# A two-block transformer kernel: a closing joined to the stage before it, and closings that begin the next stage's first products by token halves

## The reference

```
# block 1
mix = (g_a * o_a + g_b * o_b) @ w_out            # gated sum, then a product
h = h + rms_norm(mix, norm_mix_post)             # residual
hn = rms_norm(h, norm_mlp_pre)                   # input of the MLP
ff = square(relu(hn @ w_ff1)) @ w_ff2
h = h + rms_norm(ff, norm_mlp_post)
# block 2
a = rms_norm_2(h, ln_mix_pre);  proj = a @ w_in
... mix = concat(y_a, y_b, y_c, y_d) @ w_out
h = h + rms_norm_2(mix, ln_mix_post)
a = rms_norm_2(h, ln_ffn_pre)
h = h + rms_norm_2((silu(a @ w_gate) * (a @ w_up)) @ w_down, ln_ffn_post)
```

## Time and profile before

| | us |
|---|---|
| median of 3 runs (1671.85 to 1675.81) | 1674.38 |
| the profiled execution, whole | 1672.46 |
| its span, first to last instruction | 1670.6 |
| TensorE busy in the span | 1526.5 |
| VectorE busy | 813.0 |
| ScalarE busy | 572.4 |
| GpSimd busy | 284.7 |

### The profile page before, as it was taken

How to read it: one execution, slowest core, us unless ns; L and a number is a source line. 1 busy time by engine, 2 the same in 40 slices (tenths; PEclk the granted TensorE clock), 3 DMA queues, 4 the chain that set the end, 5 groups by cost and what they waited for, 6 DMA issues and landing times. The chain is left out here.

```text
span 1670.6 us, 18447 instructions
## 1 busy us (share of the span) xinstructions
PE 1526.5 (91%) x7440; PEld 1231.4 (74%) x7440; DVE 813.0 (49%) x1178; ACT 572.4 (34%) x894; POOL 284.7 (17%) x293
## 2 busy tenths in 40 slices
PE   7989699776997899999999799988798999999997
PEld 5878588664676688888887566767576888888885
DVE  4232433437753554434335597477856334334425
ACT  4221334433652441413133522176434222212212
POOL 0000000000020599100001167614322000000000
PEclk9999899887998999999999899989889999999998
DMA  4322121220013122332222312102012222222222
GB/s 170 101 77 79 51 76 45 95 76 1 1 51 113 63 91 99 101 101 102 92 88 82 101 51 77 57 26 77 1 51 76 76 99 84 95 101 101 101 88 76
DMA packets 37033, 129.23 MB, mean 77 GB/s; under 512 B 4644, under 2 KB 20924, under 8 KB 25300
## 3 DMA queue, kind: packets, MB, share of 16 engines
q1 hardware_dynamic: 36660, 127.93, 22.5%
q10 hardware_dynamic: 288, 0.12, 0.0%
HBM read 124.82 MB, written 3.17 MB: 77 GB/s over the span
## 5 line engine op out<-in xcount | busy, mean ns | idle before, releaser
L223 DVE TENSOR_TENSOR ring_lo<-ring_raw,ring_hi 128x2048 fp32r<-128x2048 f32 (+3 forms) x115 | 267.6, 2330 | 212.3 <-ACT ring_hi L213 212.2
L242 PE MATMUL bank<-xT_hi,ring_hi 128*128 128x512 f32 (+2 forms) x880 | 348.9, 397 | 5.3 <-PEq L1483 3.6
L242 PE MATMUL bank<-xT_lo,ring_hi 128*128 128x512 f32 (+2 forms) x880 | 345.7, 393 | 0.0
L242 PE MATMUL bank<-xT_hi,ring_lo 128*128 128x512 f32 (+2 forms) x880 | 345.5, 393 | 0.0
L213 ACT CAST ring_hi<-ring_raw 128x2048 fp32r<-128x2048 f32 (+3 forms) x115 | 212.7, 1852 | 254.8 <-DMA ring_raw<-in_w_ff 130.7
L242 PEld LDWEIGHTS bank<-xT_hi,ring_hi 128*128 128x128 f32 (+2 forms) x880 | 166.3, 189 | 46.8 <-issue 11.6
L242 PEld LDWEIGHTS bank<-xT_hi,ring_lo 128*128 128x128 f32 (+2 forms) x880 | 166.2, 189 | 36.5
L242 PEld LDWEIGHTS bank<-xT_lo,ring_hi 128*128 128x128 f32 (+2 forms) x880 | 166.6, 189 | 35.3
L242 PE MATMUL bank<-ring_hi,hid_hi 128*128 128x512 f32 x432 | 169.5, 392 | 3.9 <-DVE ring_lo L223 3.9
L242 PE MATMUL bank<-ring_hi,hid_lo 128*128 128x512 f32 x432 | 169.0, 391 | 0.0
L242 PE MATMUL bank<-ring_lo,hid_hi 128*128 128x512 f32 x432 | 169.0, 391 | 0.0
(11 more groups left out here) (496 smaller groups left out, 2133.0 us busy)
## 6 DMA issues: line engine op xcount, KB each, us to landing
ring_raw<-in_w_ff SPq DMA_DIRECT2D x32, 1024.0 KB, 4.8
ring_raw<-in_w_up SPq DMA_DIRECT2D x22, 1024.0 KB, 4.8
ring_raw<-in_w_proj SPq DMA_DIRECT2D x8, 1024.0 KB, 5.0
ring_raw<-in_w_gates SPq DMA_DIRECT2D x8, 1024.0 KB, 4.9
ring_raw<-in_w_fm SPq DMA_DIRECT2D x12, 512.0 KB, 4.8
ring_raw<-in_w_dn_a SPq DMA_DIRECT2D x6, 1024.0 KB, 4.9
ring_raw<-in_w_proj SPq DMA_DIRECT2D x8, 512.0 KB, 4.6
ring_raw<-in_w_out SPq DMA_DIRECT2D x4, 1024.0 KB, 5.0
```

Of the source, the lines that this page charges most:

```text
L223: k.nc.vector.tensor_tensor(k.ring.lo[:, g % SLOTS, 0:n], k.raw[:, g % SLOTS, 0:n], plain(k.ring.hi[:, g % SLOTS, 0:n]), ALU.subtract).the ...
L242: mm = k.nc.tensor.matmul(out, x, y, start=first and n == 0, stop=last and n == 3 * len(pairs) - 1)
```

## The change

Four things are done.

1. **mix1 joins the stage of the gated sum** (`stage_gemm(..., closing=closing)`), as mlp1 and mlp2 already do. The barrier between goes; in its place stand waits for the freed banks (`held`), for the first 14 taken tiles before phase one and for the last low part (`gated_low`) before phase two. SyncE's queue waits for the last taken tile before it issues S5's constants and the two gain rows. The closing's scratch tiles move to other addresses.
2. **The banks are numbered differently**: `bank(t, c)` is `2 * t + c` instead of `4 * c + t`, so that banks 0 and 1 belong to group 0 and are free first.
3. **Closings begin the next products** (`ahead`): mix1 and mix2 begin two tiles, mlp1 one tile of 96 columns. The first half of the tokens (256 columns of `xT`) of the first tile is made before `turn(2)`, that of the second before `turn(3)`; the second halves come behind `turn(3)` (and behind S5's transposes), in the same order. The next stage leaves out its first one or two steps (`begun`, `if i < 1`). For this the first two chunks of `w_ff1` are cut by columns, 256 columns over all of the depth, by two DMAs of 512 KB each, instead of 512 columns over half of it.
4. **Closings split one chunk more** before they end: ScalarE and VectorE make the parts of the next stage's second chunk inside the closing.

```diff
     def bank(self, t, c):
-        return self.k.pb[4 * c + t]
+        return self.k.pb[2 * t + c]
@@ Closing.sync
+        if after is not None:
+            sp.wait_ge(*after)
         if self.aside is not None:
             self.aside.load(sp)
-        if after is not None:
-            sp.wait_ge(*after)
@@ Closing.pe
-                        pe.wait_ge(*held[4 * c + t])
+                        pe.wait_ge(*held[2 * t + c])
...
         if self.pre is not None:
-            turn(2)
+            half = S // 2
+            if self.ahead:
+                wait_chunk(k, pe, self.end)
+                pe.wait_ge(self.low.sem, self.low.base + 4)
+            for n in range(2):
+                if n < len(self.ahead):
+                    self.begin(n, 0, half)
+                turn(2 + n)
             if self.aside is not None:
-                pe.wait_ge(self.low.sem, self.low.base + 2)
-                self.aside.turn(pe, self.bank(0, 0))
-            turn(3)
+                pe.wait_ge(self.low.sem, self.low.base + 6)
+                self.aside.turn(pe, self.bank(2, 0))
+            if self.ahead:
+                pe.wait_ge(self.low.sem, self.low.base + 8)
+            for n in range(len(self.ahead)):
+                self.begin(n, half, S).then_inc(self.ahead_done.sem, 1)
+
+    def begin(self, n, a, b):
+        _, _, out, pairs, _, _ = self.ahead[n]
+        return products(self.k, out[:, a:b], [(x, y[:, a:b]) for x, y in pairs], True, True)
@@ Closing.act, Closing.dve (at their ends)
+            if self.ahead:
+                split_hi(k, act, self.end + 2)
+            if self.ahead:
+                split_lo(k, dve, self.end + 2)
@@ first_block, the gated sum
-    stage_gemm(k, steps, gated, lambda j: "dve", act_each=split_sum, dve_tail=last_low, pool=add)
+    k.s5_in = S5Inputs(k)
+    begun, _, _ = gemm(k, g + 4, KD, 8, feature_tiles(k.xT, (0, P), 2 * P), 0)
+    closing = Closing(k, "mix1", g, ..., (134, 138, 142, 146, 120), pre=0, aside=k.s5_in,
+                      ahead=(begun, k.sig("gemm_done")),
+                      needs={(0, 0): (free.sem, free.base + KD + 6), (1, 0): (ended.sem, ended.base + 1)})
+    stage_gemm(k, steps, gated, lambda j: "dve", act_each=split_sum, dve_tail=last_low, pool=add, closing=closing)
-    g = stage_closing(k, Closing(k, "mix1", g, ..., (104, 108, 112, 116, 120), pre=0, aside=k.s5_in))
@@ stage_gemm
+                if i < begun:
+                    continue
@@ order_weights
-        whole("w_ff1", range(4 * q, 4 * q + 4))
+        if q == 0:
+            for half in range(2):
+                add_weights(k, *columns_of(d, "w_ff1", (0, 1), 4, 512, 256 * half, 256 * half + 256))
+        whole("w_ff1", range(4 * q + (2 if q == 0 else 0), 4 * q + 4))
```

More of the change, by code:

```diff
@@ L511, in stage_gemm @@
 def stage_gemm(k, steps, evac, owner=None, act_each=None, dve_each=None, dve_tail=None, pool=None,
-               needs=(), closing=None, opening=None):
+               needs=(), closing=None, opening=None, begun=0):
     nc = k.nc
@@ L1150, in __init__ @@
     def __init__(self, k, tag, g, lhs, phases, gain_name, at, pre=None, part=None, needs=None, out=None, aside=None,
-                 lead=None):
+                 ahead=None, lead=None):
         self.k, self.first, self.lhs, self.phases, self.pre = k, g, lhs, phases, pre
@@ L1155, in __init__ @@
         self.part, self.needs, self.out, self.aside = part, needs or {}, out, aside
+        self.ahead, self.ahead_done = ahead or ((), None)
         self.gain_row = k.d[gain_name]
@@ L1344, in act @@
             if self.aside is not None:
-                self.aside.keep(act, self.bank(0, 0))
+                self.aside.keep(act, self.bank(2, 0))
+            if self.ahead:
+                split_hi(k, act, self.end + 2)
     def pool(self, pool):
@@ L1701, in first_block @@
     gate_made = k.sig("gate_made")
-    free, summed, high = k.sig("gemm_free_dve"), k.sig("gated_sum"), k.sig("gated_high")
+    free, summed, high, ended = k.sig("gemm_free_dve"), k.sig("gated_sum"), k.sig("gated_high"), k.sig("gated_low")
     def low(dve, f):
@@ L1735, in last_low @@
         low(dve, KD - 2)
-        low(dve, KD - 1)
-    stage_gemm(k, steps, gated, lambda j: "dve", act_each=split_sum, dve_tail=last_low, pool=add)
+        low(dve, KD - 1).then_inc(ended.sem, 1)
+    k.s5_in = S5Inputs(k)
+    begun, _, _ = gemm(k, g + 4, KD, 8, feature_tiles(k.xT, (0, P), 2 * P), 0)
+    closing = Closing(k, "mix1", g, lambda f, t: mixT[:, f, t * P:(t + 1) * P], FULL_DEPTH, "norm_mix_post",
+                      (134, 138, 142, 146, 120), pre=0, aside=k.s5_in, ahead=(begun, k.sig("gemm_done")),
+                      needs={(0, 0): (free.sem, free.base + KD + 6), (1, 0): (ended.sem, ended.base + 1)})
+    stage_gemm(k, steps, gated, lambda j: "dve", act_each=split_sum, dve_tail=last_low, pool=add, closing=closing)
+    g = closing.end
     gate_made.base += 2 * KD
@@ L1741, in first_block @@
     high.base += KD
-    k.s5_in = S5Inputs(k)
-    g = stage_closing(k, Closing(k, "mix1", g, lambda f, t: mixT[:, f, t * P:(t + 1) * P], FULL_DEPTH, "norm_mix_post",
-                                 (104, 108, 112, 116, 120), pre=0, aside=k.s5_in))
+    ended.base += 1
     H = FF1 // P // MLP1_PARTS
@@ L1754, in first_block @@
         f0 = j
-        for _ in range(H // 4):
+        for n in range(H // 4):
+            if part == 0 and n == 0:
+                for _ in range(2):
+                    s, j, g = gemm(k, g, KD, 8, feature_tiles(k.xT, (0, P), 2 * P), j)
+                    steps += s
+                continue
             s, j, g = gemm(k, g, KD, 4, feature_tiles(k.xT, range(0, 512, P), 512), j)
@@ L1769, in first_block @@
     taken = k.sig("gemm_free_dve").base
+    begun2, _, _ = gemm(k, g + 4, KD, 8, feature_tiles(k.xT, (0,), 96, m=96), 0, range(4))
     closing = Closing(k, "mlp1", g, lambda f, t: hid[:, f, t * P:(t + 1) * P], FULL_DEPTH, "norm_mlp_post",
-                      (152, 120, 124, 156, 104), pre=1, part=y,
+                      (152, 120, 124, 156, 104), pre=1, part=y, ahead=(begun2, k.sig("proj2_done")),
                       needs={(0, 0): (k.sig("gemm_free_dve").sem, taken + up[-5] + 1),
@@ L1791, in first_block @@
     stage_gemm(k, steps, evac_ff, lambda j: "both" if tile[j][0] == "up" else "dve", needs=needs,
-               pool=s5_powers(k, er, ei, 166), closing=closing)
+               pool=s5_powers(k, er, ei, 166), closing=closing, begun=len(begun))
     k.g = closing.end
@@ L1874, in second_block @@
     end = stage_recurrent(k, side)
-    closing = Closing(k, "mix2", g, end.operand, FULL_DEPTH, "ln_mix_post_2", (184, 142, 150, 188, 196), pre=2, lead=end)
+    begun, _, _ = gemm(k, g + 4, KD, 8, feature_tiles(k.xT, (0, P), 2 * P), 0)
+    closing = Closing(k, "mix2", g, end.operand, FULL_DEPTH, "ln_mix_post_2", (184, 142, 150, 188, 196), pre=2, lead=end,
+                      ahead=(begun, k.sig("gemm_done")))
     g = stage_closing(k, closing)
@@ L1941, in second_block @@
     stage_gemm(k, steps, evac_glu, lambda j: "both" if tile[j][0] == "gate" else "dve", act_each=high_part,
-               dve_each=low_part, needs=needs, closing=closing)
+               dve_each=low_part, needs=needs, closing=closing, begun=len(begun))
     return None
@@ L2180, in _ @@
             for i, (c, j, out, pairs, start, last) in enumerate(steps):
+                if i < 1:
+                    continue
                 if c not in seen:
```

## The result

| | before | after |
|---|---|---|
| median, us | 1675.10 (1671.85 to 1683.03, 4 runs) | 1656.11 (1651.92 to 1657.22, 4 runs) |
| profiled execution, whole | 1672.46 | 1656.11 |
| its span | 1670.6 | 1654.3 |
| TensorE busy | 1526.5 | 1533.2 |

The ratio after / before is 0.9882, with a 95% interval of 0.9853 to 0.9911. The change makes the kernel faster, and the time lies in the range of the prediction (1641 to 1658), but near its upper end: between the two profiled executions 16.35 us were gained where the sum said 26.6. That is more than noise: 26.6 us off would be a ratio of 0.984, outside the interval. The question is where the other 10 us are.

What follows compares the result with a forecast made beforehand. TensorE, busy 91% of the span, was taken to bound the kernel, so time is won only where it stands or runs slowly. 11.2 + 6.5 + 6.7 + 2.2 = 26.6 us off 1672.46 gave 1645.9, forecast 1646, range 1641 to 1658.

Steps and rivals of the forecast that it cites:

- The pace: TensorE at the high level: 0.2268 us per matmul of 512 columns, 0.120 us per half of 256 columns.
- the rival of whole-priced halves: In the closings, weight loads in the open make each half cost 0.2268 us: 25.6 us lost, 1671.5, chance 0.03.
- The join, 11.2 us: Between gated sum and mix1: 11.2 us gained, 8.6 of standing and 2.6 of the low level, with no new wait.
- that rival: At the join another wait replaces the removed one, TensorE starting at about 509.5: 8.2 us lost, 1654, chance 0.08.
- mix1, 6.5 us: At mix1's end: products begun ahead gain 6.5 us, with a 1.6 us wait left and 0.7 for the barrier.
- mix2, 6.7 us: At mix2's end: the same products begun ahead gain 6.7 us, at the high level.
- mlp1, 2.2 us: At mlp1's end: one tile begun ahead gains 2.2 us, its second halves taken at the low level.
- The rival at the high level: At mlp1's end: 4.4 us gained at the high level, total 1643.7; included in the forecast's chance of 0.73.
- What the rest costs: Renumbered banks, extra splits and changed DMAs: put at nothing; one being late would cost 1 to 2 us.
- The sum: Whole kernel: the four gains add to 26.6 us off the profiled 1672.46, giving 1645.9.
- one price for the low level, in the halves and the barriers: Second halves run slowly (9.0 us) or barriers cost more (3 x 1.0): 1649 to 1658, say 1654, chance 0.14.
- one in the stages right behind the closings: Low level lasts into the next stages, each matmul costing 0.2 us more: 1681 with 25 us each, chance 0.02.

Runs made afterwards that it cites:

- e2: The changed kernel with the join and new bank numbers only, no products begun ahead in the closings: median 1663.8 us, ratio 0.9948.
- e4: The changed kernel without the join, mix1 again its own stage behind the barrier, products begun ahead kept: median 1665.9 us, ratio 0.9950.
- e11: The changed kernel with unused filling matmuls in block 2's waits, by mistake also in block 1's paired attention, and in mlp1's tail: median 1642.9 us, ratio 0.9804.
- e1: The changed kernel run again with no edit: median 1657.8 us, ratio 0.9909 to the kernel before.
- e6: The kernel before, delayed by 8 unused matmuls (1.8 us) at the start of block 1's MLP: median 1682.3 us, ratio 1.0032.
- e7: The changed kernel, delayed by 12 unused matmuls (2.7 us) at the start of the MLP stage: median 1658.9 us, ratio 0.9887.
- e8: The changed kernel with 13 filling matmuls ahead of the recurrent stage and 38 in five of its waits: median 1645.4 us, ratio 0.9813.
- e3: The changed kernel with 13 filling matmuls in the 3.1 us wait ahead of the recurrent stage: median 1655.0 us, ratio 0.9893.
- e10: The kernel before with filling matmuls in block 2's larger waits, by mistake also in block 1's paired attention: median 1679.7 us, ratio 1.0011.
- e5: The kernel before, run again with no edit: median 1672.8 us, ratio 0.9987.
- e12: e11 without the 10 + 24 filling matmuls placed by mistake in block 1's paired attention: median 1641.7 us, ratio 0.9796.

## Why the prediction was right, and where it was not

- **The pace**: 0.120 us for a half, 0.122 among the second halves, 0.2268 for a whole product. Right; the rival of whole-priced halves is out.
- **The join, 11.2 us**: 11.14, and 11.2 alone (e2). No new wait; that rival is out.
- **mix1, 6.5 us**: 6.29, and 6.6 in e4. The wait is 1.01 us behind S5's transposes, and the stage's barrier costs 0.67 (0.7 taken; 0.33 and 0.32 behind mlp1 and mix2).
- **mix2, 6.7 us**: 6.75.
- **mlp1, 2.2 us**: 2.51; the level falls there as taken. The rival at the high level was priced at 4.4: e11, which holds it by filling, has 18.55 - 13.69 = 4.9.
- **What the rest costs, nothing**: right. The only new wait for a weight split in block 1's MLP is one of 0.29 us at 671.7, and e1 has none. The 2.1 us lost there are for the most part a low stretch of 3.4 us at mlp1's first gap: e1 lacks it, and has 1.6 us of the 2.1 back.
- **The sum, 26.6 us off the profiled execution's own 1672.46**: here it failed. The terms add up to 26.69, measured. The step that was missing is that the rest of the program takes as long as before. The sum needs it, and the prediction has neither a reason nor a price for it: it takes for granted that block 2 keeps its granted clock when it moves by 20 us in time. The table shows -9.80 and -2.11 us, and e6 that a shift of 1.8 us is enough for part of it. The prediction had one price for the low level, in the halves and the barriers (1654, chance 0.14), and one in the stages right behind the closings (1681). The time came out where the first stands, 1656, but not by that mechanism: the halves and barriers cost what was forecast. That 1656.1 lies within the range is therefore luck: its upper end, 1658, was set by rivals that did not happen, and of the eight executions of the changed kernel (e1's with them) one took 1660.7.

One reading of the rows was incomplete. The prediction says that the products at 1095.62 run at the low level "though TensorE was busy"; the trace of before has a wait of 2.28 us that ends at 1094.36, a good us ahead of them. It was a first sign that a short wait in block 2 can cost a low stretch.

What stays open: why a position in time is good or bad. Before lies well in two traces out of two (284.2, 286.6) and in most of its runs; in the six traces of changed or shifted kernels without filling (after, e1, e2, e4, e6, e7) block 2 took 291.0 to 296.9 us. I could not predict a better position, and e7's delay left four of its six executions where those of after are. That the low level is the mechanism in the recurrent stage is shown by e8; which wait starts which stretch is shown at two places only (e3, e11).

## What to carry to other kernels

Add up local gains from the timeline, but before trusting the sum look at which untouched stages run partly at the low level: their time is a quantity that moves by several us when the program in front of them gets shorter, and two traces of the same kernel show how far. Where a stage alternates between waits of 1 to 5 us and short matmuls, useless matmuls into a free accumulator bank, a little shorter than each wait, can be worth more than another us of saved waiting (here some 11 us for 51 added matmuls, e8 against after, ratios 0.9813 and 0.9882 with intervals that lie apart). It isn't sure: the same kind of filling brought the kernel before little (e10, ratio 1.0011, of which the mistake's 6.7 us are 0.004). Put them only where the wait is certain, check which other stages share the code, expect a stretch saved at one place to show at the next unfilled wait, and look at the single times before you trust a median.

## What the runs showed of the hardware that I had not expected

- The same wait of 3.1 us was followed by 3.4 us at 1.2 GHz in the one kernel and by 44 us in the other, although in those 44.30 us TensorE's rows show it busy for 42.28, with the same short matmuls.
- The low level costs different amounts: about a quarter of a us per us in the recurrent stage ((83.2 - 67.6) / 62), half a us where products of 512 columns run ((63.88 - 59.40) / 9.4 in the stretch behind it, e12 against e11).
- A wait of 1.89 us ahead of mlp1's first turn was followed by the low level in after (from 894.6 to 898.1) and not in e1; of the kernel before the first trace lacks it and e5 has it (from 911.6 to 915.1). So the same kernel goes either way, and neither the wait's length nor the code decides it alone. TensorE's timeline in after, and the same row in e1:

```profile
894.20 1.59 PE L1231 MATMUL bank<-ident,cl_xn_mlp 128*128 128x128 f32 x8 [1.89 <-ACT cl_xn_mlp L1341]
```

```profile
895.01 1.09 PE L1231 MATMUL bank<-ident,cl_xn_mlp 128*128 128x128 f32 x8 [1.89 <-ACT cl_xn_mlp L1341]
```

- The executions of one kernel differ by 10 us and more, and the time goes with the mean granted clock: beside e5, the kernel before took 1670.5 to 1672.2 us at 0.950 to 0.951 and 1682.9 to 1684.8 at 0.942 to 0.944.
- A half-product of 256 columns loads the same weights again and still costs 0.120 us, 0.007 more than half a whole one.
